# Recurrent layer of a two-block transformer kernel: input products of steps 2 to 4 made as merged units in alternating bank pairs, with the down product between them

## What is computed

```python
def rg_lru(u, gate_w, gate_b, lam):
    g = jnp.einsum('bshi,hio->bsho', uh, gate_w) + gate_b
    g = jax.nn.sigmoid(g.astype(jnp.float32))
    ...
    log_a = -LRU_C * r * jax.nn.softplus(-lam.astype(jnp.float32))
    a = jnp.exp(log_a)
    mult = jnp.sqrt(-jnp.expm1(2.0 * log_a))
    bterm = mult * (i * u.astype(jnp.float32))
    # h_t = a_t * h_(t-1) + bterm_t

def recurrent_mixer(h, w_in, conv_w, conv_b, gate_w, gate_b, lam, w_out):
    u = jnp.einsum('bsd,dc->bsc', h, w_in)
    gate, xb = u[..., :WIDTH], u[..., WIDTH:]
    xb = causal_depthwise_conv(xb, conv_w, conv_b)
    y = rg_lru(xb, gate_w, gate_b, lam)
    return jnp.einsum('bsc,cd->bsd', y * jax.nn.silu(gate), w_out)
```

## Time and profile before

| | us |
|---|---|
| median of 3 runs | 861.24 (860.34 to 861.68) |
| the profiled execution, its time | 861.02 |
| its span, first to last instruction | 858.6 |
| PE busy | 848.0 |
| DVE busy | 677.3 |
| ACT busy | 542.2 |
| POOL busy | 39.8 |

### The profile page before, as it was taken

One profiled execution on the slowest core, in us unless ns is written; L12 is line 12 of the kernel. 1 busy time (PEld: TensorE's weight loads), 2 busy tenths in 40 slices (PEclk: granted clock), 3 DMA queues, 4 the chain that ended last, 5 costly groups with the idle time before them and its releaser, 6 DMA issues.

```text
span 858.6 us, 13362 instructions
## 1 busy us (share of the span) xinstructions
PE 848.0 (99%) x4881; PEld 746.6 (87%) x4881; DVE 677.3 (79%) x970; ACT 542.2 (63%) x746; POOL 39.8 (5%) x57
## 2 busy tenths in 40 slices
PE   8999999999999999999999999999999999999997
PEld 8988789888888888889888888889999898888886
DVE  6899868887878798868887886787987877776764
ACT  5855656757556566576666656578988664555533
POOL 1000100000000041000000000000010100000000
PEclk9999999999999999999999999999999999999999
DMA  7654534675654344224666655435364046545511
GB/s 276 228 194 152 178 139 151 236 236 206 215 210 161 145 179 164 99 99 149 244 218 245 224 203 208 151 133 210 137 241 163 0 149 245 214 184 212 219 50 49
DMA packets 22908, 152.80 MB, mean 178 GB/s; under 512 B 2608, under 2 KB 2736, under 8 KB 5712
## 3 DMA queue, kind: packets, MB, share of 16 engines
q1 hardware_dynamic: 22176, 149.45, 47.9%
q0 software_dynamic: 544, 2.49, 0.9%
q10 hardware_dynamic: 144, 0.26, 0.1%
HBM read 151.14 MB, written 1.05 MB: 177 GB/s over the span
## 4 chain that ended last, share of the span: by engine, by line
PE 94%; DVE 2%; DMA 1%; ACT 1%; issue 1%; POOL 0%; ACTq 0%; SPq 0%; DVEq 0%; POOLq 0%
PE ring L1798 36%; PE acc L1862 31%; PE ring L1847 10%; PE ring L1809 3%; PE acc L2085 3%; PE ring L1933 1%; PE ring L1828 1%; PE ring L2067 1%; DMA raw<-in_stream_dram 1%; PE acc L1756 1%; PE ring L2243 1%; PE ring L2125 1%; PE ring L1912 1%; DVE w_lo L1004 1%; PE ring L2145 0%
## 5 line engine op out<-in xcount | busy, mean ns | idle before, releaser
L1004 DVE TENSOR_TENSOR w_lo<-raw,w_hi 128x2048 fp32r<-128x2048 f32 (+1 forms) x145 | 318.0, 2197 | 6.7 <-ACT w_hi L511 6.6
L511 ACT ACTIVATE w_hi<-raw 128x2048 fp32r<-128x2048 f32 (+1 forms) x146 | 266.9, 1840 | 52.6 <-DMA raw<-in_stream_dram 49.4
L1798 PE MATMUL ring<-hh,w_hi 128*128 128x512 f32 x944 | 223.9, 390 | 0.0
L1798 PEld LDWEIGHTS ring<-hh,w_hi 128*128 128x128 f32 x944 | 175.2, 188 | 35.1
L1798 PEld LDWEIGHTS ring<-hh,w_lo 128*128 128x128 f32 x944 | 117.4, 192 | 2.7 <-DVE usum L1122 0.3
L1798 PE MATMUL ring<-hh,w_lo 128*128 128x256 f32 x944 | 118.4, 283 | 0.1
L1862 PE MATMUL acc<-w_hi,a_hi 128*128 128x512 f32 x264 | 103.6, 392 | 0.0
L1862 PE MATMUL acc<-w_lo,a_hi 128*128 128x512 f32 x264 | 102.8, 389 | 0.0
L1862 PE MATMUL acc<-w_hi,a_lo 128*128 128x512 f32 x264 | 102.8, 389 | 0.0
L1122 DVE TENSOR_TENSOR usum<-ring,usum 128x512 f32<-128x512 f32 x65 | 44.7, 688 | 55.3 <-ACT usum L516 55.3
L1847 PE MATMUL ring<-hh,w_hi 128*128 128x256 f32 x480 | 87.8, 285 | 0.0
(11 more groups left out here) (247 smaller groups left out, 963.1 us busy)
## 6 DMA issues: line engine op xcount, KB each, us to landing
raw<-in_stream_dram SPq DMA_DIRECT2D x134, 1024.0 KB, 4.8
raw<-in_stream_dram SPq DMA_DIRECT2D x12, 512.0 KB, 3.9
gatew<-in_gatew_dram POOLq DMA_DIRECT2D x4, 384.0 KB, 4.2
x<-in_x_dram SPq DMA_DIRECT2D x2, 512.0 KB, 3.7
out_dram<-xn SPq DMA_DIRECT2D x3, 256.0 KB, 2.6
row<-in_row_dram POOLq DMA_DIRECT2D x1, 640.0 KB, 5.0
gup_raw<-in_gup_dram SPq DMA_DIRECT2D x3, 128.0 KB, 11.2
par<-in_par_dram SPq DMA_DIRECT2D x1, 274.0 KB, 4.5
```

Of the source, the lines that this page charges most:

```text
L511: nc.scalar.activation(w_hi[:, u % RING, 0:n], raw[:, u % RAW, 0:n], ACT.Copy).then_inc(hi_split, 1)
L1004: nc.vector.tensor_tensor(w_lo[:, u % RING, 0:n], raw[:, u % RAW, 0:n], w_hi[:, u % RING, 0:n].bitcast(f32), ALU.subtract).then_inc(lo_spl ...
L1798: last = nc.tensor.matmul(into, w_parts[part][:, u % RING, lo:lo + P], moving(kc), start=(n, kc) == (0, 0), stop=(n, kc) == (1, KC - 1), s ...
```

## The change

Input units of steps 2, 3 and 4 are made by `merged` instead of `wide`. Step j uses the bank pair j % 2 (banks 0 and 1, or 2 and 3) for x, then for the heads of that step (a step later), and for g between them; the other pair belongs to the neighbouring steps. In steps 1 and 5 x and g stay wide, in banks 0 and 2, and 2 and 3. Since a merged result has two parts, ACT and DVE add them for x (`branch_summed`) and for g (`lru_gate_summed`), as step 0 did already.

PE's order in steps 2 to 4 becomes x, heads, down, g, and the units of the stream follow. ACT takes `act_high` ahead of the second group of splits and the gate's tanh behind it; DVE takes `act_low` ahead of the second group too. The product (sgate + 1) * gate of steps 2 to 4 goes from DVE to POOL, as an addition and a multiplication behind the clamp of the step before.

```diff
@@ lru_plan
-        for kind, e in (("x", j), ("g", j), ("d", j - 2)):
+        x, g, d = ("x", j), ("g", j), ("d", j - 2)
+        for kind, e in (x, d, g) if j < LRU_ITERS - 1 else (x, g, d):
@@
-BRANCH_BANK, GATE_BANK, HEAD_BANKS = 0, 2, (1, 3)
+MERGED_STEPS = range(2, LRU_ITERS - 1)
+BRANCH_BANK, GATE_BANK = {1: 0, LRU_ITERS - 1: 2}, {1: 2, LRU_ITERS - 1: 3}
+def step_pair(j):
+    return j % 2
+def head_bank(e, k):
+    return (1, 3)[k] if e == 0 else k + (2 if e % 2 and e < LRU_ITERS - 1 else 0)
@@ POOL
                 nc.gpsimd.tensor_scalar(ug[:, :, :], ug[:, :, :], 0.0, None, ALU.max).then_inc(clamped, 1)
+                j = e + 1
+                if j in MERGED_STEPS:
+                    pool.wait_ge(gate_ready, STEP_LRU + j + 1)
+                    own.mark(nc.gpsimd.tensor_scalar(sgate[:, :, :], sgate[:, :, :], 1.0, None, ALU.add))
+                    own.wait()
+                    nc.gpsimd.tensor_tensor(gg[:, j % 2, :, :], sgate[:, :, :], gg[:, j % 2, :, :], ALU.mult).then_inc(gate_free, 1)
@@ ACT, branch_taken
+                if j not in BRANCH_BANK:
+                    b = 2 * step_pair(j)
+                    nc.scalar.activation(xb[:, :, :], ring[:, b:b + 2, S:2 * S], ACT.Copy).then_inc(branch_crossed, 1)
@@ ACT, gated
+                if j not in GATE_BANK:
+                    if j > 1:
+                        act.wait_ge(act_ready, STEP_LRU + j - 1)
+                    b = 2 if j == 0 else 2 * step_pair(j)
+                    nc.scalar.activation(gg[:, j % 2, :, :], ring[:, b:b + 2, S:2 * S], ACT.Copy).then_inc(gate_crossed, 1)
+                    act.wait_ge(gate_summed, j + 1 - (j > 1))
+                    gate = gg[:, j % 2, :, :]
@@ ACT, the loop over steps
-                if j >= 2:
+                if j == LRU_ITERS - 1:
                     gated(j)
-                for u in plan[1]:
-                    split(u)
-                if j == LRU_ITERS - 1:
                     last_gates(j)
                 elif j:
                     act_high(e)
+                for u in plan[1]:
+                    split(u)
+                if j in MERGED_STEPS:
+                    gated(j)
@@ DVE
+            def branch_summed(j):
+                b = 2 * step_pair(j)
+                dve.wait_ge(branch_crossed, j + 1 - (j > 1))
+                nc.vector.tensor_tensor(xb[:, :, :], ring[:, b:b + 2, 0:S], xb[:, :, :], ALU.add).then_inc(branch_free, 1)
+            def lru_gate_summed(j):
+                b = 2 if j == 0 else 2 * step_pair(j)
+                dve.wait_ge(gate_crossed, j + 1 - (j > 1))
+                nc.vector.tensor_tensor(gg[:, j % 2, :, :], ring[:, b:b + 2, 0:S], gg[:, j % 2, :, :], ALU.add).then_inc(gate_summed, 1)
@@ DVE, the loop over steps
+                if j not in BRANCH_BANK:
+                    branch_summed(j)
                 if j:
                     inputs_gated(e)
                 lru_conv(j)
...
-                if j >= 2:
                     lru_gate(j)
+                if 0 < j < LRU_ITERS - 1:
+                    act_low(e)
+                if j in MERGED_STEPS:
+                    lru_gate_summed(j)
                 for u in plan[1]:
                     split(u)
-                if 0 < j < LRU_ITERS - 1:
-                    act_low(e)
@@ PE, gates
+                elif e == 1:
+                    pe.wait_ge(gate_free, 2)
                 else:
-                    pe.wait_ge(gate_summed, 1)
+                    pe.wait_ge(gate_summed, e + 1 - (e > 1))
@@ PE, the loop over steps
-                if j:
-                    wide(LRU_UNIT["x", j], BRANCH_BANK, free=(branch_free, j))
+                if j in BRANCH_BANK:
+                    wide(LRU_UNIT["x", j], BRANCH_BANK[j], free=(branch_free, 1) if j == 1 else (ri_ready, 2 * j - 2))
                     gates(j - 1)
-                    wide(LRU_UNIT["g", j], GATE_BANK, free=(gate_free, j))
+                    wide(LRU_UNIT["g", j], GATE_BANK[j], free=(gate_summed, 1))
+                elif j:
+                    merged(LRU_UNIT["x", j], step_pair(j), free=(ri_ready, 2 * j - 2), low_first=True)
+                    gates(j - 1)
+                    lru_down(j - 2)
+                    merged(LRU_UNIT["g", j], step_pair(j), free=(branch_free, j + 1), low_first=False)
```

More of the change, by code:

```diff
@@ L831, in gates @@
                         c = 2 * (2 * e + k) + r
-                        last = nc.scalar.activation(buf[:, k, :], ring[:, HEAD_BANKS[k], r * S:(r + 1) * S],
+                        last = nc.scalar.activation(buf[:, k, :], ring[:, head_bank(e, k), r * S:(r + 1) * S],
                                                     ACT.Tanh, scale=0.5, bias=half_bias[:, c:c + 1])
@@ L882, in gated @@
                 act.wait_ge(used, LRU_UNIT["g", j] + 1)
[L883 to L886, removed]
-                else:
+                if j not in GATE_BANK:
[5 more added lines that the diff above has]
+                    gate = gg[:, j % 2, :, :]
+                else:
+                    gate = ring[:, GATE_BANK[j], :].rearrange("p (k s) -> p k s", k=2)
+                if j:
                     act.wait_ge(gate_free, j)
-                    gate = ring[:, GATE_BANK, :].rearrange("p (k s) -> p k s", k=2)
                 nc.scalar.activation(sgate[:, :, :], gate, ACT.Tanh, scale=0.5).then_inc(gate_ready, 1)
@@ L1587, in recurrence @@
                 nc.vector.tensor_tensor(actl[:, :, :], yy[:, :, :], gg[:, e % 2, :, :], ALU.mult).then_inc(act_ready, 1)
+            def lru_gate_summed(j):
+                b = 2 if j == 0 else 2 * step_pair(j)
+                dve.wait_ge(gate_crossed, j + 1 - (j > 1))
+                nc.vector.tensor_tensor(gg[:, j % 2, :, :], ring[:, b:b + 2, 0:S], gg[:, j % 2, :, :], ALU.add).then_inc(gate_summed, 1)
             def lru_gate(j):
-                if j == 0:
-                    dve.wait_ge(gate_crossed, 1)
-                    nc.vector.tensor_tensor(gg[:, 0, :, :], ring[:, 2:4, 0:S], gg[:, 0, :, :], ALU.add).then_inc(gate_summed, 1)
+                if j not in GATE_BANK:
                     dve.wait_ge(gate_summed, 1)
-                    gate = gg[:, 0, :, :]
+                    gate = gg[:, j % 2, :, :]
                 else:
@@ L1598, in lru_gate @@
                         dve.wait_ge(act_ready, STEP_LRU + j - 1)
-                    gate = two(GATE_BANK)
+                    gate = two(GATE_BANK[j])
                 dve.wait_ge(gate_ready, STEP_LRU + j + 1)
@@ L1784, in has_low_of, with merged @@
                     pe.wait_ge(h_lo_ready, lows + 4 * t + kc // 2 + 2)
-            def merged(u, k, i=0, done=None):
+            def merged(u, k, i=0, done=None, free=None, low_first=None):
                 ready(u, i)
@@ L1790, in merged @@
                     pe.wait_ge(summed, done)
-                order = (0, 1) if k == 0 else (1, 0)
+                if free is not None:
+                    pe.wait_ge(*free)
+                order = (1, 0) if (k == 1 if low_first is None else low_first) else (0, 1)
                 for n, part in enumerate(order):
@@ L2236, in gates @@
                 pe.wait_ge(conv_ready, e + 1)
-                if e:
+                if e == LRU_ITERS - 1:
                     pe.wait_ge(ri_ready, 2 * e)
+                elif e == 1:
+                    pe.wait_ge(gate_free, 2)
                 else:
-                    pe.wait_ge(gate_summed, 1)
+                    pe.wait_ge(gate_summed, e + 1 - (e > 1))
                 for k in range(2):
                     for r in range(2):
-                        last = nc.tensor.matmul(ring[:, HEAD_BANKS[k], r * S:(r + 1) * S],
+                        last = nc.tensor.matmul(ring[:, head_bank(e, k), r * S:(r + 1) * S],
                                                 gatew[:, 2 * e + k, r * P:(r + 1) * P], xc[:, k, :],
```

15 lines of the change are left out of this document (6 added, 9 removed).

## The result

| | before | after |
|---|---|---|
| median of six runs each, us | 861.32 (860.34 to 861.68) | 865.25 (864.25 to 866.53) |
| profiled execution, us | 861.02 | 865.61 |
| its span, us | 858.6 | 863.8 |
| mean granted clock | 0.999 (profiled execution) | 0.994 to 0.997 (six runs) |

The ratio is 1.0048, with a 95% interval of 1.0037 to 1.0058: slower by 3.9 us, where 3.2 was forecast, and inside the range. The trace shows where. From the start of the first heads (step 1) to the sum into x that ends the layer, the kernel before takes 679.05 - 588.35 = 90.70 us and the changed one 683.11 - 588.69 = 94.42, so 3.72 of it lie in this stage.

What follows compares the result with a forecast made beforehand. PE alone was taken to bound the kernel. Merged units -1.2, the wait for a_lo +3.4 and the late convolution +1.0 summed to +3.2 us on a median of 861.24, so 864.4, range 862.5 to 867.0.

Steps and rivals of the forecast that it cites:

- What bounds: Recurrent layer: PE alone sets the time, busy 99% of the span; the last convolution ends 0.17 us before its heads.
- Merged units, -1.2: Input units of steps 2 to 4: 32 matmuls instead of 48, 0.20 us less each, six units.
- The wait for a_lo, +3.4: Step 2, first down product: PE waits about 3.5 us for DVE's a_lo, up to 0.17 of it already paid.
- On the path, since nothing later has slack to give back: Step 2's a_lo wait counts in full, +3.4 us; in steps 3 and 4 a_lo costs nothing.
- The clock: PE's granted clock, full in every slice of the profile; the forecast sum has no term for its falling.
- the rival: PE's clock falls in the a_lo wait, costing 2.7 us and hiding the late convolution: 866.1 us; chance 11%.
- a dent in the granted clock: One of the signs listed beforehand that would show the prediction wrong; no size was given.
- POOL, +1.0 at the last heads: POOL's product delays DVE's gated input 0.7 us a step, 1.2 in step 5; PE waits 1.0 for the convolution.
- 17.4 forecast: Period in us of the ACT and DVE loop per step, unless POOL slows it, against 18.29 of PE.
- Full lock: POOL's product and clamp both run before DVE's gated input, 2.2 us a step: 868.9 us; chance 7%.
- first, third and fifth: POOL disturbs nothing, 863.4 us (19%); clock falls in the wait, 866.1 (11%); units don't get shorter, 865.6 (6%).
- The likeliest case: Whole kernel: the main forecast of 864.4 us (863.6 to 865.5), given 47%.

Runs made afterwards that it cites:

- e1: The changed kernel plus 14 extra 512-column matmuls ahead of the first down product, keeping PE busy in its wait for a_lo; 864.28 us, 1.0048 times the kernel before.
- e7: The changed kernel with step 2 left as in the kernel before, only steps 3 and 4 merged, bank pairs exchanged; 862.52 us, 1.0015 times the kernel before.
- e9: The changed kernel with step 2 as before, steps 3 and 4 merged, and their gate product on DVE instead of POOL; 860.30 us, 0.9998 times before.
- e4: The kernel before with only the new order and the moved a_hi and a_lo; units wide, gate product on DVE; 867.00 us, 1.0072 times before.
- e8: The changed kernel with one weight split moved from step 0 to step 1; 866.20 us, 1.0066 times the kernel before.
- e3: The changed kernel with the gate product of steps 2 to 4 back on DVE, behind the second group of splits; 865.90 us, 1.0065 times before.
- e6: The changed kernel itself run again, on the chip of the second set; 866.19 us, 1.0055 times the kernel before.

## Why the prediction was right, and where its working was off

- *What bounds.* PE alone, with 0.17 us between the convolution and the last heads. e1 and e7 waited at just that place, and e9 came within 0.05 of it. Right.
- *Merged units, -1.2.* 11.11 instead of 11.51 a pair, seen in after and, by their absence, in e4. Right.
- *The wait for a_lo, +3.4.* 3.16 in the trace, at 606.8 on an axis that runs 0.34 late: PE waited 3.2. That is a little under the 3.3 to 3.5 that it had named, and right; e4 and e7 show that it is the order in step 2 that makes it.
- *"On the path, since nothing later has slack to give back".* Right for the kernel as it was changed: in steps 3 and 4 there is no wait, as said. But the wait was not worth its whole length once it was made smaller, since the loop of ACT and DVE then came last (e1, e8).
- *The clock.* The working took it as full; the rival had it fall with 11%. It fell, and the prediction had named a dent in the granted clock as a sign that it was wrong. This is the step that failed: the sum lacks +1.65, and the rival's price of 2.7 (the middle between 0 and a whole down unit at half clock) was 1.0 too high, because the clock came back after about 3 us. With 1.65 in its place the rival gives 861.2 + 2.2 + 1.65 = 865.1, against 865.25. e1 shows the link: with PE busy in the same 3.2 us the down product has 5.69. Windows of 1 us over the whole trace of before do show a full clock up to the last matmul, but its longest wait of PE was 1.47.
- *POOL, +1.0 at the last heads.* In after it did not come, and the rival said that it would be hidden. In e1, the clock's share away, it came: 0.8. Its parts were somewhat too high: 0.50 a step instead of 0.7, and 0.92 in step 5 instead of 1.2. The loop without POOL is 17.53 (17.4 forecast), with it 18.04.
- *Full lock.* The price of 2.2 a step appears nowhere. The gated input beside POOL's product was 0.50 longer in a step, and 1.10 at most (e7, step 5), since the clamp starts behind the gated input and not ahead of it. The Trainium skill, "SBUF — State Buffer", section "Who interferes with whom", has whoever issues first hold the pair for a whole instruction; for the product the trace comes near it (in e1 the gated input ended 0.54 after the product, where a full block would make it 0.69), for the clamp in the earlier trace rows it does not, where the gated input ended 0.34 before the clamp's row. POOL's spans are rough, and the runs do not tell these apart.

The range's sentence has a slip: the fourth rival, the full lock at 868.9, lies outside 862.5 to 867.0, so the range takes in the middle cases of the first, third and fifth.

The forecast of 864.4 came within 0.9 of 865.25 for a sum with one term that did not show (+1.0) and one that was left out (+1.65). That the two nearly cancel is luck; the wait and the units are not. What happened is -1.2 + 3.2 + 1.65 = +3.65, against 3.72 in the stage. The likeliest case was not quite what happened; the rival with 11% was, nearly term by term. The rule of the Trainium skill, "TensorE: Matmul & The Clock Gate", section "HAM oscillation", that gaps between matmul groups can put the clock back, deserved more than its 11%, and the trace agrees with it (0.50 behind a wait of 3.16). A full clock in a trace whose longest wait is 1.47, and which has none in this layer, says little on what a wait of 3 us does.

## What to carry to other kernels

Where PE is busy throughout, price a new wait at its length plus what the matmuls behind it may lose at the lower clock (here 3.2 + 1.65), and look for the dent in windows of about 1 us, not in the slices of a page. Before moving a consumer ahead on the critical engine, compute its producer's time to the tenth, and compare the period of the helper engines' loop with that of PE: savings on PE alone stop where the two meet (here 18.3 against 18.0, or 17.5 without POOL). And when a fix gives back less than its term, look for the next wait at once: a stall hides others, and e1 seemed useless only because it uncovered one.

## What was unexpected of the hardware

- Waits of 2.9 to 3.2 us after gapless matmuls (after, e3, e4, e6), and in one run each of 2.45 and 1.95, brought the granted clock to 0.50 for some 3 us; one of 1.74 did not. A wait of 1.5 did in two profiled executions of eleven. In e8 the window behind the wait still had 1.00, and the fall came about 1 us into the down product.
- A POOL product of two 128x512 SBUF operands has a row of 2.86 us, but ended 1.16 after DVE's split of 128x2048 did, so most of its row was waiting, by this reading. POOL's addition has 2.26 beside a split; the clamp, of the same size and kind, has 1.49 in the earlier trace rows. An engine with 6% busy time lengthened the loop of another by 0.5 us a step.
